# Fourier block of a two-block network: the sine features go first and the shift is added to column 0 ahead of the cosine features

## The reference, cut to what matters

```python
def modulate(h, g, shift, scale):
    return rms_norm(h, g) * (1 + scale) + shift

def fourier_mix(a, w_out):
    B, L, D = a.shape
    ag = a.reshape(B, L, FNET_GROUPS, FNET_GROUP_DIM).astype(jnp.float32)
    f = jnp.fft.fft2(ag, axes=(1, 3), norm="ortho").real
    return f.astype(a.dtype).reshape(B, L, D) @ w_out

sh1, sc1, gt1, sh2, sc2, gt2 = ada_params(c, w_mod[i], b_mod[i])   # silu(c) @ w_mod + b_mod, six parts
h_lat = h_lat + gt1 * fourier_mix(modulate(h_lat, g_norm_mix[i], sh1, sc1), w_fnet_out)
h_lat = h_lat + gt2 * conv_ffn(modulate(h_lat, g_norm_ffn[i], sh2, sc2), ...)
```

## Time and profile before

| what | value |
|---|---|
| median of 3 runs | 1522.35 us (1522.3 to 1522.35) |
| the profiled execution's own time | 1522.58 us |
| its span, first to last instruction | 1520.8 us |
| PE, DVE, ACT, POOL busy | 99%, 69%, 42%, 67% |
| mean granted clock of TensorE | 0.996 |
| DMA, mean over the span | 118 GB/s |
| DMA, first two of 40 slices | 376 and 404 GB/s |

### The profile page before, as it was taken

How to read it: one execution, slowest core, us unless ns; L and a number is a source line. 1 busy time by engine, 2 the same in 40 slices (tenths; PEclk the granted TensorE clock), 3 DMA queues, 4 the chain that set the end, 5 groups by cost and what they waited for, 6 DMA issues and landing times.

```text
span 1520.8 us, 26991 instructions
## 1 busy us (share of the span) xinstructions
PE 1500.8 (99%) x9405; PEld 1359.0 (89%) x9405; DVE 1045.7 (69%) x1605; ACT 634.3 (42%) x1142; POOL 1012.5 (67%) x802
## 2 busy tenths in 40 slices
PE   8999999999999999999999999999999999999997
PEld 7898999998887899999888888888888999999897
DVE  7877777873428477766943667676457787777954
ACT  6443566650113355565122213232235555554442
POOL 4735877766666777776764647566466787776684
PEclk9999999999999999999999999999999999999999
DMA  9942333344233334445342232322232333332332
GB/s 376 404 151 72 103 104 97 103 151 160 97 111 87 94 112 118 119 126 152 95 124 69 84 109 83 119 73 83 70 97 84 97 111 103 103 110 86 94 114 69
DMA packets 236237, 179.24 MB, mean 118 GB/s; under 512 B 5376, under 2 KB 214528, under 8 KB 235776
## 3 DMA queue, kind: packets, MB, share of 16 engines
q1 hardware_dynamic: 234864, 171.91, 36.4%
q10 hardware_dynamic: 1296, 6.29, 1.2%
HBM read 172.94 MB, written 5.24 MB: 117 GB/s over the span
## 4 chain that ended last, share of the span: by engine, by line
PE 57%; DVE 5%; issue 2%; POOL 2%; ACT 1%; DMA 1%; POOLq 0%; DVEq 0%; ACTq 0%
PE ps L1077 19%; PE ps L1080 19%; PE ps L1081 19%; DMA raw<-in_w_ff_up 1%; POOL tmp L931 1%; POOL w_lo L949 0%; POOL tmp L940 0%; DVE wide_lo L3132 0%; DVE ps L3118 0%; DVE act_lo L3126 0%; DVE ps L3119 0%; DVE ps L3120 0%; DVE tmp L3117 0%; PE ps L1512 0%; DVE gates_r L3126 0%
## 5 line engine op out<-in xcount | busy, mean ns | idle before, releaser
L1077 PE MATMUL ps<-act_hi,w_hi 128*128 128x256 f32 (+1 forms) x864 | 284.0, 329 | 2.9 <-ACT gates L1898 1.3
L917 POOL TENSOR_TENSOR w_lo<-raw,w_hi 128x1024 fp32r<-128x1024 f32 x110 | 274.6, 2497 | 9.2
L1080 PE MATMUL ps<-act_hi,w_lo 128*128 128x256 f32 (+1 forms) x864 | 280.4, 325 | 0.0
L1081 PE MATMUL ps<-act_lo,w_hi 128*128 128x256 f32 (+1 forms) x864 | 280.3, 324 | 0.0
L1077 PE MATMUL ps<-wide_hi,w_hi 128*128 128x512 f32 (+2 forms) x733 | 261.1, 356 | 1.5 <-POOL w_lo L917 0.6
L1080 PE MATMUL ps<-wide_hi,w_lo 128*128 128x512 f32 (+2 forms) x733 | 260.4, 355 | 0.0
L1081 PE MATMUL ps<-wide_lo,w_hi 128*128 128x512 f32 (+2 forms) x733 | 260.4, 355 | 0.0
L914 POOL TENSOR_TENSOR w_hi<-raw,zero 128x1 fp32r<-128x1 f32 x110 | 30.1, 273 | 261.3 <-PE ps L1077 260.4
L949 POOL TENSOR_TENSOR w_lo<-raw,w_hi 128x512 fp32r<-128x512 f32 x128 | 165.5, 1303 | 52.5 <-ACT w_hi L1646 51.9
L1077 PEld LDWEIGHTS ps<-act_hi,w_hi 128*128 128x128 f32 x864 | 165.5, 192 | 19.6 <-issue 3.2
L1080 PEld LDWEIGHTS ps<-act_hi,w_lo 128*128 128x128 f32 x864 | 165.6, 192 | 13.9 <-issue 1.4
(11 more groups left out here) (325 smaller groups left out, 3956.4 us busy)
## 6 DMA issues: line engine op xcount, KB each, us to landing
raw<-in_w_in SPq DMA_DIRECT2D x88, 512.0 KB, 4.1
gates<-in_w_mod_t SPq DMA_DIRECT2D x20, 1024.0 KB, 10.4
raw<-in_w_ffn_up SPq DMA_DIRECT2D x40, 512.0 KB, 3.8
raw<-in_w_ffn_down SPq DMA_DIRECT2D x22, 512.0 KB, 3.5
raw<-in_w_ff_gate SPq DMA_DIRECT2D x22, 512.0 KB, 3.8
raw<-in_w_ff_up SPq DMA_DIRECT2D x22, 512.0 KB, 3.8
raw<-in_w_r_out SPq DMA_DIRECT2D x16, 512.0 KB, 3.4
raw<-in_w_ff_down SPq DMA_DIRECT2D x16, 512.0 KB, 3.8
```

What stands on the lines that cost most here:

```text
L917: nc.gpsimd.tensor_tensor(w_lo[:, two, :], raw[:, slot, :], f32(w_hi[:, two, :]), SUB).then_inc(split_done, 1)
L1077: ins = mm(o, w, a, start=start, stop=False)
L1080: mm(o, wl, a, start=False, stop=False)
L1081: return mm(o, w, al, start=False, stop=stop)
```

## The change

The sine products of all eight tiles go first, each pair sharing one PSUM bank. Then TensorE waits for `mean_ready`: DVE's new `shift_columns` has added the shift to column 0 of the transformed tiles u and split it again. Then come the eight cosine products, which now carry the shift. The 128x1 matmuls and their splits go. The lo part of tiles 6 and 7 moves from POOL to DVE (`f_lo`), and `fnet_panel(3)` loses its wait. `shift_chunk([2, 3])` is issued ahead of `fnet_panel(0)`, and the second `fnet_lo` of POOL, two more `shift_sum` and a second `fnet_hi` of ACT come ahead of the f tiles. The first two output tiles are done together, block by block, 512 columns wide.

```diff
-F_BANK = (4, 6, 2)
-DC_SUMMED, DC_DONE, DC_HI_MADE, DC_READY = 1, 2, 3, 4
+F_BANK = (6, 7, 4)
+SINE_BANK = (4, 5, 2, 3)
+F_POOL = 6
...
         def f_odd(m):
-            return ps[:, F_BANK[m % 3] + 1, :]
+            return ps[:, SINE_BANK[m // 2], HALVES[m % 2]]
... SP
             shift_chunk([0, 1])
+            shift_chunk([2, 3])
             fnet_panel(0)
-            shift_chunk([2, 3])
...
             sp.wait_ge(dft_split, TT + 1)
-            sp.wait_ge(dc_step, DC_DONE)
             fnet_panel(3)
... GpSimd
             fnet_lo(0)
-            for m in range(KT):
+            fnet_lo(1)
+            for m in range(F_POOL):
                 pool.wait_ge(f_hi_made, m + 1)
                 pool.wait_ge(mod_step, mod_done(0, SHIFT_POOL + m // 2))
-                nc.gpsimd.tensor_tensor(act_lo[:, m, 1:], f_tile(m)[:, 1:], f32(act_hi[:, m, 1:]), SUB).then_inc(f_ready, 1)
+                nc.gpsimd.tensor_tensor(act_lo[:, m, :], f_tile(m), f32(act_hi[:, m, :]), SUB).then_inc(f_ready, 1)
... TensorE
-            for m in range(3):
-                pe.wait_ge(u_made, 2 * m + 4)
-                features(f_odd(m), m, 1, half, half)
-            for m in range(3):
+            for m in range(KT):
+                pe.wait_ge(u_made, (3, 4, 7, 8)[m // 2])
+                features(f_odd(m), m, 1, half, half).then_inc(u_done, 1)
+            pe.wait_ge(mean_ready, 1)
+            for m in range(KT):
+                if m == 2:
+                    pe.wait_ge(f_q_copied, 2)
+                if m >= 3:
+                    pe.wait_ge(f_made, 3 * (m - 2))
                 features(f_even(m), m, 0, 0, half + 2).then_inc(f_done, 1)
-            for m in range(3, KT):
-                pe.wait_ge(f_made, 3 * (m - 2))
-                features(f_even(m), m, 0, 0, half + 2)
-                features(f_odd(m), m, 1, half, half).then_inc(f_done, 1)
-            pe.wait_ge(f_made, 3 * (KT - 2))
-            pe.wait_ge(dc_step, DC_SUMMED)
-            for m in range(KT):
-                ...
-                    ins = mm(dc_psum[:, m:m + 1], raw[:, 2, c0:c0 + P], udc[:, 2 * g + k:2 * g + k + 1], start=k == 0, stop=k == 1)
...
-            for n, (m, t_) in enumerate(FNET_TILES):
+            for n in range(2):
+                pe.wait_ge(fnet_split, n + 1)
+                pe.wait_ge(f_q_copied, 6 + 2 * n)
+            for b in range(KT):
+                if b < F_POOL:
+                    pe.wait_ge(f_ready, b + 1)
+                else:
+                    pe.wait_ge(mean_ready, 2 + b - F_POOL)
+                for n in range(2):
+                    ins = product(ps[:, FNET_BANKS[n], :], *w_block(fnet_weights(n), b), act_hi[:, b, :], act_lo[:, b, :],
+                                  b == 0, b == KT - 1)
+                    ...
+            for n, (m, t_) in list(enumerate(FNET_TILES))[2:]:
                 if n >= FNET_RING:
                     pe.wait_ge(fnet_free, n - FNET_RING + 1)
                 pe.wait_ge(fnet_split, m + 1)
-                if n == 0:
-                    ...
... ScalarE
                 if m == 6:
+                    shift_sum(1)
                     fnet_hi(0)
-            shift_sum(1)
             shift_sum(2)
+            shift_sum(3)
+            fnet_hi(1)
...
             for m in range(KT):
-                act.wait_ge(f_done, m + 1)
+                act.wait_ge(u_done, KT + m // 2 * 2 + 2)
                 if m >= 2:
                     act.wait_ge(f_made, 3 * (m - 1))
...
-            fnet_hi(1)
-            act.wait_ge(dc_step, DC_DONE)
-            do(dc_column(act_hi), dc_psum, ACT.Identity).then_inc(dc_step, 1)
... VectorE
             u_lo(6)
+            mod_tiles(0, range(4, 6))
             u_lo(7)
-            mod_tiles(0, range(4, 6))
+            mod_tiles(0, range(6, 8))
...
-                for m in range(KT):
-                    ins = ts(udc[:, m:m + 1], lo[:, m:m + 1], hi[:, m:m + 1], shift_dc[:, m:m + 1], ADD, ADD)
-                ins.then_inc(dc_step, 1)
+                link(tt(mean_dc, f32(lo), shift_dc, ADD))
+                link(tt(mean_dc, mean_dc, f32(hi), ADD))
+                link(ts(hi, mean_dc, 1.0, None, MUL))
+                tt(lo, mean_dc, f32(hi), SUB).then_inc(mean_ready, 1)
+            def f_lo(m):
+                dve.wait_ge(f_hi_made, m + 1)
+                tt(act_lo[:, m, :], f_tile(m), f32(act_hi[:, m, :]), SUB).then_inc(mean_ready, 1)
+            shift_columns()
...
                 dve.wait_ge(f_q_copied, m + 1)
+                dve.wait_ge(f_done, m + 1)
...
-                if m < 2:
-                    mod_tile(0, 6 + m)
-                if m == 3:
-                    shift_columns()
+            for m in range(F_POOL, KT):
+                f_lo(m)
             mod_tiles(2, range(2))
```

More of the change, by code:

```diff
@@ L289, in build @@
         early = tmp[:, 4, :]
-        dec, silu_c, gain_mix, shift_dc, udc = (early[:, EARLY + 8 * i:EARLY + 8 * (i + 1)] for i in range(5))
+        dec, silu_c, gain_mix, shift_dc, mean_dc = (early[:, EARLY + 8 * i:EARLY + 8 * (i + 1)] for i in range(5))
         lgt = early[:, EARLY + 40:EARLY + 80].rearrange("p (i n) -> p i n", i=5)
@@ L491, in build @@
         EIGHT_GATE_BANK = (4, 5, 4, 5, 2, 3)
-        dc_psum = ps[:, 3, 0:KT]
         def dc_column(w):
@@ L540, in build @@
         u_done, u_copied, u_hi_made, u_made = (sem(n) for n in ("u_done", "u_copied", "u_hi_made", "u_made"))
-        dc_step = sem("dc_step")
+        mean_ready = sem("mean_ready")
         f_done, f_q_copied, f_made, f_hi_made, f_ready = (
@@ L893, in fnet_add @@
                 nc.gpsimd.tensor_tensor(tmp[:, 0, t_], tmp[:, 0, t_], tmp[:, 1, t_], ADD).then_inc(squares_added[0], 1)
-            for m in range(1, 6):
+            for m in range(2, 6):
                 fnet_lo(m)
@@ L1144, in _ @@
             pe.wait_ge(dft_split, TT + 1)
-            for m in range(3):
-                pe.wait_ge(u_made, 2 * m + 4)
-                features(f_odd(m), m, 1, half, half)
-            for m in range(3):
-                features(f_even(m), m, 0, 0, half + 2).then_inc(f_done, 1)
-            for m in range(3, KT):
-                pe.wait_ge(f_made, 3 * (m - 2))
-                features(f_even(m), m, 0, 0, half + 2)
-                features(f_odd(m), m, 1, half, half).then_inc(f_done, 1)
-            pe.wait_ge(f_made, 3 * (KT - 2))
-            pe.wait_ge(dc_step, DC_SUMMED)
-            for m in range(KT):
-                g, e = m // 2, m % 2
-                for k in range(2):
-                    c0 = k * 2 * GROUP + e * P
-                    ins = mm(dc_psum[:, m:m + 1], raw[:, 2, c0:c0 + P], udc[:, 2 * g + k:2 * g + k + 1], start=k == 0, stop=k == 1)
-            ins.then_inc(dc_step, 1)
+            for m in range(KT):
[7 more added lines that the diff above has]
+                    pe.wait_ge(f_made, 3 * (m - 2))
+                features(f_even(m), m, 0, 0, half + 2).then_inc(f_done, 1)
             halves = HALVES
@@ L1173, in half_sums @@
                 mm(ps[:, bank, halves[i]], ones[:, :], tmp[:, 1, halves[i]], start=False, stop=True).then_inc(norm_summed[0], 1)
-            for n, (m, t_) in enumerate(FNET_TILES):
+            for n in range(2):
[9 more added lines that the diff above has]
+                                  b == 0, b == KT - 1)
+                    if b == KT - 1:
+                        ins.then_inc(fnet_done, 1)
+            for n, (m, t_) in list(enumerate(FNET_TILES))[2:]:
                 if n >= FNET_RING:
@@ L1711, in f_hi @@
                 act.wait_ge(shift_summed, m // 2 + 1)
-                hi_of(act_hi[:, m, 1:], f_tile(m)[:, 1:], f_hi_made)
-                if m == 0:
-                    shift_sum(3)
+                hi_of(act_hi[:, m, :], f_tile(m), f_hi_made)
             for m in range(KT):
-                act.wait_ge(f_done, m + 1)
+                act.wait_ge(u_done, KT + m // 2 * 2 + 2)
                 if m >= 2:
                     act.wait_ge(f_made, 3 * (m - 1))
-                do(f_sine(m), f_odd(m)[:, 0:T // 2], ACT.Identity).then_inc(f_q_copied, 1)
+                do(f_sine(m), f_odd(m), ACT.Identity).then_inc(f_q_copied, 1)
                 if m:
@@ L2429, in shift_columns @@
                 dve.wait_ge(mod_step, mod_done(0, KT - 1))
-                hi, lo = (f32(dc_column(w[:, S_U:S_U + KT, :])) for w in (wide_hi, wide_lo))
-                for m in range(KT):
-                    ins = ts(udc[:, m:m + 1], lo[:, m:m + 1], hi[:, m:m + 1], shift_dc[:, m:m + 1], ADD, ADD)
-                ins.then_inc(dc_step, 1)
+                hi, lo = (dc_column(w[:, S_U:S_U + KT, :]) for w in (wide_hi, wide_lo))
+                link(tt(mean_dc, f32(lo), shift_dc, ADD))
[6 more added lines that the diff above has]
+            shift_columns()
             half = T // 2
@@ L2440, in _ @@
                 dve.wait_ge(f_q_copied, m + 1)
+                dve.wait_ge(f_done, m + 1)
                 tt(f[:, 1:half], even[:, 1:half], odd[:, 1:half], SUB).then_inc(f_made, 1)
```

(12 more changed lines are left out.)

## The result

The changed kernel takes 1527.84 us, the median of 7 runs (1526.91 to 1528.59); the kernel before, measured beside it, 1522.36 (7 runs, 1522.30 to 1522.46). The ratio is 1.0035, 95% interval 1.0025 to 1.0044: slower by 5.5 us, above the predicted range. The profiled execution has a span of 1526.5 us against 1520.8 and a mean granted clock of 0.994 against 0.996.

The account below looks back on a forecast made before the run. TensorE, busy 99%, and squares behind a full DMA queue bound it; the 5.1 us lead becomes a wait. Queue +0.3 and clock fall 2.3 put the second sum 1.45 later: 1522.35 + 1.45 = 1523.8 us, range 1521.9 to 1525.3.

Parts of the forecast that it names:

- case 1: TensorE's lead becomes a wait before the first sum over squares and the clock falls in it: 1523.8 us, 50%.
- case 3: DMA queue runs dry at SP's wait for the first two part-2 tiles: slower, about 1525.5 us, 12%.
- the prediction's own sign: Prediction wrong if TensorE does not wait before the first sum over squares, or that sum starts before 92.3 or after 94.
- the cost of `shift_columns`: VectorE's four linked operations before the cosine products: about 0.2 us each, 0.8 to 1.6 in all; mean_ready about 41.7.
- Output tiles at 49.4: First two output tiles start at 49.4, once tile 7's sine copy frees the bank, and end at 60.3, 5.1 us ahead.
- case 2: Clock stays up behind the wait, or falls already in the cosine phase; only +0.3 is left: 1522.65 us, 33%.
- The queue's shift of 0.3: SP's first part-4 chunk issues at 55.2, not 52.48; later loads shift 0.2 to 0.3 us, bounds 0 to 1.3.
- The prediction's 4.6 us: Estimated landing time after issue of one megabyte at 400 GB/s, with about 2.0 us fixed cost per transfer.
- Where the lead goes: Before the first sum over squares nearly all of the 5.1 us lead becomes a wait for ACT's squares.
- The fall of the clock in the standstill: TensorE's 4.35 us standstill before the first sum over squares lowers the clock, costing 2.3 us, bounds 0 to 3.3.
- Panel 0 at 36.0: fnet_panel(0), sent behind two more megabytes, lands at 36.0; ACT's fnet_hi(0) then runs 36.0 to 37.1.
- without slack: From ACT's second w_up_first panel at 81.77, ACT and POOL alternate with no spare time until the last square at 92.5.

Follow-up runs that it names:

- Taking GpSimd away: Changed kernel with GpSimd's second panel lo part waiting until shift_columns is done; 1524.73 us, ratio 1.0015.
- both repairs: Changed kernel with VectorE's first two part-2 modulation tiles moved early and GpSimd's second panel lo part behind shift_columns; 1522.46 us, ratio 1.0000.
- the filled wait: Changed kernel with 36 extra unused 256-column matmuls ahead of the first sum over squares; 1527.02 us, ratio 1.0029.
- the hole mended: Changed kernel with VectorE's first two part-2 modulation tiles moved early, behind shift_columns and f tile 5; 1523.33 us, ratio 1.0005.
- the first panel early: Changed kernel with fnet_panel(0) issued ahead of shift_chunk([2, 3]) again, as in the kernel before; 1525.94 us, ratio 1.0020.
- the sum one tile later: Changed kernel with the first sum over squares moved one tile later, behind tile 10; 1527.52 us, ratio 1.0030.

## Why the prediction was wrong

The forecast was case 1; what came is the mechanism of case 3, which had 12%, together with the clock's fall of case 1. The clock cost somewhat more than priced, the queue over ten times as much. By the prediction's own sign, a first sum later than 94, it was wrong: the sum came at 96.68.

- **The step that failed is the cost of `shift_columns`**: "these cost about 0.2 each, an estimate from that row's 0.19 per operation; the links could double it (0.8 to 1.6)". The links cost what I said: three took 0.17 us. The first took 2.33, and my upper bound of 1.6 for all four did not hold it (2.95). The row I took it from is of an operation with one input tensor, which GpSimd does not block, and its 0.19 is the distance from one to the next, not the length of one (0.26). I looked only at what VectorE has queued, not at what GpSimd runs at that moment. By my own times ACT's part of panel 0 was ready at 37.1, and behind it GpSimd had two lo parts of 2.4 us to make, the second over just this spot. With the operation blocked, mean_ready came at 43.7 instead of 41.7, and TensorE waited 3.18 us instead of 1.5. Taking GpSimd away gives 0.17, a wait of 1.10 and 1524.73 us, which the predicted range holds.
- **Output tiles at 49.4**: 52.52, because of that wait and because the clock fell behind it (0.60, 0.54), which I had as a bound of the lead and as a chance of case 2. Without the collision they start at 50.0, with the wait for the sine copy as the last one, as forecast.
- **The queue's shift of 0.3, bounds 0 to 1.3**: it was 4.1. The place was right ("SP's wait for the first two tiles of part 2"), and so was the rule that each microsecond is paid in full: in the traces with an issue at 55.25, 56.53, 57.79, 58.15 and 58.65 us ACT takes the second `w_up_first` panel at 83.40, 84.69, 85.91, 86.18 and 86.76, 28.0 to 28.2 later each time. But the payment starts where that line meets 81.77, at about 53.6, and not at my 55.0; the 3 us that I gave the queue in store were not there. The input was off as well: the tiles were to end at 55.2, SP issued at 57.79. With the collision away SP issues at 55.25, my 55.2, and this chunk takes 4.9 us, my 4.7, and lands at 60.15, 0.45 late. And yet the second `w_up_first` panel comes 1.6 us late: this term was mis-sized too. I had measured by the landing of one load. In the kernel before, the loads issued at 54.04 and 54.88 (SyncE's timeline) were on their way beside it; in the other there was nothing. What later loads pay is about the missing transfer time, 1.4 us, not the first landing. The prediction's 4.6 us from the Trainium skill rests on a fixed cost that the page DMA: Bandwidth & Descriptors, section Anatomy of one DMA, gives for the path of DMAs issued by GpSimd; these loads, issued by SyncE, took 4.9 us here and 4.8 in the changed kernel.
- **Where the lead goes**: held. In the changed kernel and in every experiment in which GpSimd's order ahead of the squares stood as it was, the first sum waits for ACT's last square; with both repairs 4 us of lead leave the second sum at 106.09, where it was.
- **The fall of the clock in the standstill**: held in its kind (4.88 us, then 0.50), and roughly in size: 2.5 us of work lost where I had 2.3, and 1.6 at the second sum, where my cases 1 and 2 lie 1.15 apart (107.54 and 106.39). In the time of the whole program the filled wait shows 0.8 of it, not clear of noise. With both repairs the standstill is 2.78 us and the fall costs 0.5. With the hole mended and the cosine phase late, TensorE waits 1.02 us, the clock stays up, and the time is 1523.3.
- **Case 3 was given 12% and put at 1525.5.** That was 2.9 us above case 2 and 1.7 above case 1. In the traces 4.1 of queue and 1.6 of clock make the 5.7 by which the second sum and the end of the span are late. I had counted three queues chained behind one panel in its favour and still gave the collision no place in the price of the first operation.
- **Panel 0 at 36.0** came at 35.8, and u_lo(7), expected ready at 38.5, ended at 38.2 (VectorE's timeline of the changed kernel: 37.47 and 0.75).

That the lead could be had by an edit I had not looked for, GpSimd's order ahead of the squares, says that "without slack" was true of the chain as written, not of what it must do.

## What to carry to other kernels

Before an elementwise step is put on a critical path at the price of a similar row, look at what GpSimd runs beside VectorE in that moment, and count the SBUF inputs of both: an operation of 0.17 us took 2.33 here, as long as its neighbour's. Where a DMA queue is full, every issue that waits for an engine's late work is priced by when the queue runs dry, and from there each microsecond was paid in full here; put the work that frees the next issue ahead of work that nobody waits for. A lead of the main engine is worth only what the next joint lets through, so look first at what is ready there and whether its own order can be changed.

## What the runs showed of the hardware

- A VectorE tensor_tensor of 128x8 with two SBUF inputs took 0.17 us beside an idle GpSimd and 2.29 to 2.34 us, in five profiles, beside GpSimd's tensor_tensor of 128x1024 (2.34 to 2.36 us) that had begun 0.02 to 0.09 us before it; both ended together each time. It was blocked wholly, not slowed in share. One of 128x8 with one input in PSUM took 0.17 us beside the same GpSimd operation.
- The granted clock fell in or behind TensorE's gaps of 4.88, 4.85, 3.79, 3.78, 3.29, 3.18, 2.78 and 2.41 us, and not at those of 1.39 us and less. Of two of 1.8 us it fell behind one, in the cosine phase with the first panel early (0.55 from 42 to 44), and not behind the other, ahead of the sum one tile later: the gap alone does not decide.
- Where a hole opened in the saturated DMA queue, a panel that is taken 28 us behind the late issue was late by about the missing transfer time: 1.6 us for 1.4, 2.9 for 2.6 (the first panel ahead of the shift chunks), 4.1 for 3.9.
- The changed kernel's runs spread by 1.7 us and those of the kernel before, measured beside it, by 0.16; in the later series the latter spread by 0.6 to 1.8. What sets the spread was not tried.
